# Layer-1 query and gate projections as 2x2 block products with seven half-products, keys and values through DRAM

## What is computed

```python
def window_gqa_layer(h_lat, h_ctx, w_in, sink, w_out, with_ctx_out):
    z = h_lat @ w_in                                  # 1024 x 1024 by 1024 x 2560
    q, k, v, g = z[..., :o1], z[..., o1:o2], z[..., o2:o3], z[..., o3:]
    q = axial_rope(q, cos_r, sin_r, cos_c, sin_c)
    k = axial_rope(k, cos_r, sin_r, cos_c, sin_c)
    zc = h_ctx @ w_in[:, o1:o3]                       # keys and values of the context
    ...                                               # scores in a window, softmax with a sink
    y_lat = (o * jax.nn.silu(g)) @ w_out
```

## Times and profile before

| | |
|---|---|
| three runs | 1406.67, 1405.72, 1405.45 us, median 1405.72 |
| profiled execution | span 1402.8 us from first to last instruction (no other time is listed for it) |
| TensorE | 1357.6 us busy, 97% |
| VectorE, ScalarE, GpSimd | 866.7, 730.4, 522.0 us busy |
| projections of layer 1 | 839.3 to 1072.5 us of the span |
| attention begins | 1076.2 us |

### The profile page before, as it was taken

How to read it: one execution, slowest core, us unless ns; L and a number is a source line. 1 busy time by engine, 2 the same in 40 slices (tenths; PEclk the granted TensorE clock), 3 DMA queues, 4 the chain that set the end, 5 groups by cost and what they waited for, 6 DMA issues and landing times. The chain is left out here.

```text
span 1402.8 us, 20174 instructions
## 1 busy us (share of the span) xinstructions
PE 1357.6 (97%) x7212; PEld 1153.9 (82%) x7212; DVE 866.7 (62%) x1250; ACT 730.4 (52%) x1150; POOL 522.0 (37%) x251
## 2 busy tenths in 40 slices
PE   5999999999999999999999999999998999999998
PEld 4788888888888888878888888888886788888786
DVE  7788968686868686892211154222213899998732
ACT  6475747474747474763222242222222899999421
POOL 0022222222232323212552533345433666667542
PEclk9999999999999999999999999999999999999999
DMA  9423131313131313264424443644357333242693
GB/s 373 155 89 119 61 103 60 103 60 103 60 103 60 103 60 103 87 229 151 135 90 135 158 157 114 157 135 124 101 153 222 124 100 98 82 142 68 193 269 116
DMA packets 94056, 177.18 MB, mean 126 GB/s; under 512 B 10384, under 2 KB 56496, under 8 KB 91696
## 3 DMA queue, kind: packets, MB, share of 16 engines
q1 hardware_dynamic: 94000, 176.44, 39.0%
HBM read 122.40 MB, written 44.06 MB: 119 GB/s over the span
## 5 line engine op out<-in xcount | busy, mean ns | idle before, releaser
L1031 PE MATMUL slab<-h_hi,w_hi 128*128 128x512 f32 x720 | 256.4, 356 | 3.0 <-DVE h_lo L372 2.3
L1032 PE MATMUL slab<-h_lo,w_hi 128*128 128x512 f32 x720 | 255.7, 355 | 0.0
L1033 PE MATMUL slab<-h_hi,w_lo 128*128 128x512 f32 x720 | 255.3, 355 | 0.0
L1003 POOL TENSOR_TENSOR w_lo<-wraw,w_hi 128x1024 fp32r<-128x1024 f32 x29 | 78.3, 2699 | 300.6 <-ACT w_hi L623 300.6
L2363 POOL TENSOR_TENSOR probs<-probs,rdenom 128x2560 f32<-128x2560 f32 (+1 forms) x32 | 135.7, 4242 | 53.6 <-DVE rdenom L2311 53.6
L1031 PEld LDWEIGHTS slab<-h_hi,w_hi 128*128 128x128 f32 x720 | 136.5, 190 | 22.9 <-DVE h_lo L372 2.6
L1033 PEld LDWEIGHTS slab<-h_hi,w_lo 128*128 128x128 f32 x720 | 136.5, 190 | 19.2
L1032 PEld LDWEIGHTS slab<-h_lo,w_hi 128*128 128x128 f32 x720 | 136.6, 190 | 18.9
L2000 PE MATMUL slab<-h_hi_c,w_hi 128*128 128x512 f32 x320 | 124.9, 390 | 0.5 <-POOL w_lo L1960 0.5
L2002 PE MATMUL slab<-h_hi_c,w_lo 128*128 128x512 f32 x320 | 124.5, 389 | 0.0
L2001 PE MATMUL slab<-h_lo_c,w_hi 128*128 128x512 f32 x320 | 124.5, 389 | 0.0
(11 more groups left out here) (345 smaller groups left out, 3189.6 us busy)
## 6 DMA issues: line engine op xcount, KB each, us to landing
wraw<-in_w_in SPq DMA_DIRECT2D x32, 512.0 KB, 3.4
wm<-in_wm SPq DMA_DIRECT2D x32, 512.0 KB, 3.6
mixT<-work SPq DMA_DIRECT2D x16, 640.0 KB, 4.0
wm<-in_wm SPq DMA_DIRECT2D x8, 1024.0 KB, 17.4
mraw<-mixT SPq DMA_DIRECT2D x16, 512.0 KB, 6.1
q_parts<-qT SPq DMA_DIRECT2D x32, 256.0 KB, 4.6
oT<-o_out SPq DMA_DIRECT2D x8, 1024.0 KB, 5.2
work<-in_xT SPq DMA_DIRECT2D x8, 640.0 KB, 8.3
```

Source lines behind the costliest of these rows:

```text
L1031: nc.tensor.matmul(out, l_hi, r_hi, start=start, stop=False)
L1032: nc.tensor.matmul(out, l_hi, r_lo, start=False, stop=False)
L1033: return nc.tensor.matmul(out, l_lo, r_hi, start=False, stop=stop)
```

## The change

**What it does.** The query and gate weights are taken in eight pairs of slabs (four of queries, four of gates). A pair is a 2x2 matrix of blocks: 2 slabs by 2 halves of the 1024 input features. h of the latents is one too: 2 halves of features by 2 halves of the tokens. Of the eight half-products (one block by one half: 4 tiles of features, 512 tokens, 12 matmuls) seven are made, in the order A11, A12, S2, S1, S3, S4, A22. Their operands are sums: on the weights' side S3 = A11-A21, S2 = A22-S3, S1 = S2+A11, S4 = A12-S2 for each pair; on h's side four sums T (16 pieces of 128x512 once). All sums are on GpSimd; each of the seven blocks and each T is split into hi (ScalarE) and lo (VectorE; before, GpSimd made the lo of weights).

TensorE adds products up in three PSUM banks of a pair; partial results are needed between two products, so ScalarE copies a bank (`take`) while TensorE waits with the next product into that bank, and VectorE adds other banks to the copies (`add_product`). The four results of a pair (each 128x512) are rotated, split and stored, or gated and stored, in halves.

Values come first now (slabs 0 and 1), are transposed group by group and stored to DRAM (`v`); attention fetches all of its values from there, the context's once, each block's window in turn. Keys are rotated after that and stored to DRAM (`kT`); `kd_hi`, `kd_lo` are loaded from it by 8 DMAs in pair 5 and 8 in pair 6. Before attention only block 0's queries are loaded. Buffers lie at other places.

**The core of the diff** (lines between the pieces are left out):

```diff
+        def half(p, i):
...
+            pe.wait_ge(bl.sem, bl.at + 7 * p + i + 1)
...
+            elif i == S2:
+                pe.wait_ge(cp.sem, cp.at + 4 * p + 1)
+                if p == 0:
+                    pe.wait_ge(tl.sem, tl.at + 16)
+            elif i == S3:
+                pe.wait_ge(cp.sem, cp.at + 4 * p + 2)
+            elif i == S4:
+                pe.wait_ge(cp.sem, cp.at + 4 * p + 3)
+            elif i == A22:
+                pe.wait_ge(cs.sem, cs.at + 3 * p + 2)
...
+        for p in range(PAIRS):
+            for i in (A11, A12, S2, S1, S3, S4, A22):
+                half(p, i)
```

ScalarE (`take` ends with cp, `finish_half` is the hi of a rotated half or a gate's tanh):

```diff
+        def take(k, bank, product):
+            p, j = k // 4, k % 4
+            act.wait_ge(pp.sem, pp.at + 7 * p + product)
...
+            else:
+                act.wait_ge(gst[j // 2], 32 * (p - Q_PAIRS))
...
+            for n in range(12, 16):
+                t_hi(n)
+            evict(2, 1)
...
+            for p in range(PAIRS):
+                more = p + 1 < PAIRS
+                k = 4 * p
+                if p > Q_PAIRS:
+                    finish_half(k - 2)
+                if p > 0:
+                    take(k - 1, 0, 7)
+                    block_hi(p, A22)
+                take(k, 0, 1)
+                if p == 0:
+                    rotated_hi(0)
...
+                if more:
+                    block_hi(p + 1, A12)
+                take(k + 2, 0, 3)
+                if more:
+                    block_hi(p + 1, S2)
+                if p == 0:
+                    rotated_hi(1)
+                finish_half(k)
+                take(k + 1, 1, 4)
```

VectorE and GpSimd:

```diff
+            for p in range(PAIRS):
...
+                block_lo(p, A22)
+                if p > 0:
+                    begin_half(k - 1)
+                    end_half(k - 1)
+                if more:
+                    block_lo(p + 1, A11)
+                if p == 0:
+                    rotate(1)
+                add_product(k, 2, 2, 1)
+                begin_half(k)
+                if more:
+                    block_lo(p + 1, A12)
+                if p == 0:
+                    add_rotated(1)
+                end_half(k)
...
+            sines(0)
+            rotated_lo(0)
+            sines(1)
+            for p in range(PAIRS):
...
+                if more:
+                    third_sum(p + 1)
+                if p == 0:
+                    second_sum(1)
+                    rotated_lo(1)
+                half_sines(k)
```

SyncE (KD_AT = 5; `load_x` waits for the lo of S4 of the pair before, `load_y` for that of A22):

```diff
+            for p in range(PAIRS):
+                if p + 1 < PAIRS:
+                    load_y(p + 1)
...
+                store_half(4 * p)
...
+                if p + 2 < PAIRS:
+                    load_x(p + 2)
+                if p in (KD_AT, KD_AT + 1):
+                    load_kd(p - KD_AT)
+                if p == QB_AT:
+                    load_first_block()
+                store_half(4 * p + 1)
```

Attention:

```diff
-                v = vs[:, LT + x - left, u, :]
...
+                v = v_ctx[:, x - left, u, :] if x >= left else vw[:, s, x, u, :]
```

More of the change, by code:

```diff
@@ L126, in out0_home, with laid_over @@
     return Home0(early, wo_a, junk, wo_b, mraw, x1, hb, m0, st, eps, wo_c, xn, xt, wo_d, gpb, m1, Y, TP)
-Home1 = namedtuple("Home1", "c_hi c_lo w_hi w_lo G kd_hi kd_lo wraw1 hraw2 C Z H R L vs slab VP q mask sink ident")
+Home1 = namedtuple("Home1", "c0_hi c0_lo c1 x_hi x_lo w_hi w_lo w_blocks t_parts kd_hi kd_lo wraw1 hraw2 raw_a vg C Z CK ZK R4 "
+                            "R_kv HK LK HQ LQ TG third slab VP q mask sink ident")
+def laid_over(nc, *buffers):
+    with ExitStack() as ctx:
+        return [ctx.enter_context(nc.sbuf_tensor(name, shape, dt)) for name, shape, dt in buffers]
 def proj1_home(nc):
+    KH = KT // 2
+    block, half = [P, 2, KH, P], [P, 512]
     with ExitStack() as ctx:
@@ new lines, in banks, with half_of, result, rotated @@
+    def banks(p):
+        return [slab[:, 3 * (p % 2) + i, :] for i in range(3)]
+    def half_of(k):
+        m, t = HALVES[k % 4]
+        return k // 4, 2 * (k // 4 % Q_PAIRS) + m, t
+    def result(k):
+        return home1.R4[:, k % 4, :] if k < 4 * Q_PAIRS else gates[:, k % 4, :]
+    def rotated(n):
+        if n < 2:
+            return R_kv[n][:, 0:N_LAT], CK[:], ZK[:], cos, sin
+        p, m, t = half_of(n - 2)
+        return result(n - 2), C[:, n % 2, :], Z[:, n % 2, :], cos[:, t * 512:(t + 1) * 512], sin[:, t * 512:(t + 1) * 512]
@@ new lines, in gate @@
+        def gate(k):
+            p, j = k // 4, k % 4
+            g = k - 4 * Q_PAIRS
+            if j == 3:
+                act.wait_ge(cp.sem, cp.at + k + 1)
+            else:
+                act.wait_ge(cs.sem, cs.at + 3 * p + j + 1)
+            if g < 2:
+                for done in qst:
+                    act.wait_ge(done.sem, done.at + 16 * 4 * Q_PAIRS)
+            else:
+                act.wait_ge(gg.sem, gg.at + g - 1)
+            nc.scalar.activation(TG[:, k % 2, :], result(k), ACT.Tanh, scale=0.5).then_inc(gt.sem, 1)
@@ L2200, in body @@
                 if is_block(b, NB - 3):
-                    sp.wait_ge(gst, 16 * KT)
+                    for stored in gst:
+                        sp.wait_ge(stored, 16 * KT)
                     sp.wait_ge(ost_s[0], 16)
```

834 lines of the change are left out of this document (553 added, 281 removed).

## The result

The changed kernel takes **1466.6 us** (median of 4 runs, 1465.2 to 1469.8), the kernel before 1405.6 on the same chip: a ratio of 1.0436 with a 95% interval of 1.0421 to 1.0450, 61 us slower. The forecast was 1455 with a range of 1421 to 1476. The profiled execution has a span of 1463.3 us, 60.5 above the 1402.8 of before.

What follows compares the result with a forecast made beforehand. TensorE, busy 97% of the span, was taken to bound the kernel. 71.3 us of added waits and costs less 21.7 of removed products gave +49.6; 1402.8 + 49.6 + 2.9 = 1455 us, range 1421 to 1476.

Steps and rivals of the forecast that it cites:

- before pair 0: Sums T and their lows ahead of the first query pair: 4 us of added time (0 to 8).
- pair 0 with its part of the clock: First query pair: TensorE waits 18.9 us at S4 for the copy after S1; a lower clock adds 2.8 us.
- pairs 1 to 3: Other query pairs: 27.2 us each, 8.2 over the 19.0 of products, three times: 24.6 us added.
- pair 4, pair 5: First two gate pairs: 7 us as the first copy waits for the last query sine, then 2 us.
- pairs 6 and 7: Last two gate pairs: copies wait for gate stores issued behind 8 key loads, 8 us and then 3 us.
- rival C: Query pairs: clock stays low (+11) or weight loads take longer behind two stores per query half; 1470 us, chance 0.13.
- The exclusion: Query pairs: GpSimd and two-SBUF-input VectorE instructions hold each other up, sharing one time, 15.5 + 9.0 = 24.5 us a pair.
- rival A: Projection pairs: VectorE and GpSimd are hardly held because they meet seldom; +17, 1423 us, chance 0.14.
- The 2.7 us that I added on top for the load of the second slab: Query pairs after the first: GpSimd's sums wait for the second weight slab, making 24.5 us into 27.2.
- 25.6; a gate store lands in 5.0 us, copy 0.6: Second-last gate pair: store issued behind key loads at 25.6 us, copy possible at 31.2, against 24.4 wanted: 6.8 us late.
- Cost 0: Attention: value windows from DRAM are as large and asked for as early as the SBUF transfers replaced; 0 us added.
- B: Projection pairs: GpSimd's half-size instructions take 0.9 us, copies come within their cover, gain kept; 1387 us, chance 0.05.

## Why the prediction was right, and where it was off

Measured against its own terms, from the stretches above (19.0 us a pair; sum 49.6 predicted, 60.5 measured):

| term | predicted | measured |
|---|---|---|
| removed | -21.7 | -21.7 |
| before pair 0 | 4 | 3.5 (62.7 against 59.2) |
| pair 0 with its part of the clock | 18.9 + 2.8 | 21.8 |
| pairs 1 to 3 | 24.6 | 19.4 |
| pair 4, pair 5 | 7, 2 | 5.8, 1.1 |
| pairs 6 and 7 | 8 + 3 | 26.2 |
| end of the projections | 1 | 0.7 |
| attention | 0 | 5.7 |

The measured terms add to 62.5; the keys' first product started 1.9 us earlier in this execution (837.33 against 839.27), which no term covers, and the last 0.1 is rounding. The 59.2 are the 233.1 us of all projections before, less the 173.9 of the queries and gates.

That the sum came so near is partly luck. Two terms were 20.9 us too small (pairs 6 and 7, attention) and five others together 8.1 too large, most of it in pairs 1 to 3. The measured 1466.6 is also nearer to rival C's 1470 than to the forecast's 1455; C's cause is answered below. TensorE's idle time from the first projection product to the last was forecast near 70 us; it is 58.0, and 20 more are products at the lower clock.

**The exclusion was right.** It decides the size and not the sign: pairs 1 to 3 lost 19.4 of the 60.5 us, and rival A, without it, was slower too. The rows, read in another part of the program, held in the pairs. The cuts of sines and of lows took 3.9 and 2.8 us a pair, the move of sines to VectorE 1.8, the early copies by themselves nothing. 24.5 us of shared time were counted, and the pairs took 25.5 on average (24.6, 26.8, 25.0). The 2.7 us that I added on top for the load of the second slab were the step that was too large: GpSimd waited for no transfer in pairs 1 to 3, only for VectorE's shuffles (20.0 us) and ScalarE's high parts (3.9). The count itself is a little high too: the shared instructions were under way for 23.0 us a pair, because one engine's follows the other's more closely than their lengths alone say (the addition above ended 0.54 us after the sum). The Trainium skill's rule (SBUF — State Buffer, section SBUF: two separate sides) says the same, for the two-input instructions of VectorE; the trace agrees, with VectorE's 1.53 to 1.83 us for a 128x512 beside GpSimd against 0.68, while additions that read PSUM kept to 0.68 and shuffles to 0.73.

**Pair 0 was right**: S4 started 32.7 us after A11, forecast 32.5, behind the copy after S1, itself behind the first query half's hi; the slow products behind the wait cost 2.7 us, forecast 2.8. The wait alone is 16.64 us and not 18.9, because the products ahead of it took longer: A11, at the lower clock behind a wait of 3.16 us, 4.43 us instead of 2.72. What the chain consists of was shown in part: moving the keys' and the halves' sines to VectorE took 7.4 us, cutting the halves' sines alone nothing that can be told.

**Pairs 6 and 7 were off by 15 us.** The step that failed: "25.6; a gate store lands in 5.0 us, copy 0.6". I priced the keys ahead of the store by their issue (0.96 us each from the earlier trace rows, an issue time of another form of DMA; here 0.6) and then let the store land as if the queues were empty. Its bytes stood behind 2.56 MB, 10.9 us at the 235 GB/s or so that the queues moved while the keys passed. Spreading the loads, which changes no issue time, took 19.5 us out of the two pairs; issuing the store first took out nothing. Pair 7 I took for a smaller case of the same, 3 us, although mask and first queries stand there behind the second 8 loads; it was the same again, 11.7. And each long wait drew products at the lower clock: of the 26.2 us 20.2 are waits and 6.0 are slow products; I had this in pair 0 only.

**Attention was off by 5.7 us.** The step that failed: "Cost 0". I weighed what the window's transfer costs and how early it is asked for, and not what its new place on SyncE holds up: at block NB - 3 the wait for products of values now stands ahead of the mixed tiles' load, which is issued at 1314.5 us where GpSimd wants the tiles at 1318.3 (1324.14 less the 5.87 of its wait). The order of SyncE's issues in attention's last blocks was to be read, as it was for the key loads in pair 5.

**The clock** lay as predicted in time that is waited for, in pairs 1 to 3: keeping it up changed 76.42 us to 76.16. In pairs 6 and 7, where a transfer sets the wait, no run kept it up, so whether the 6.0 us would come back there is open. Rival A (hardly held) and B (gain kept) are refuted by the pairs' 25.5 us; rival C named the clock and slower weight loads, and neither is the cause: between the stores of query halves the loads of 512 KB landed in 4.0 and 4.9 us, sooner than before. Its 1470 was near the time for another reason, the gate stores.

## What to carry to other kernels

Before work is taken off a TensorE that is busy all the time and given to VectorE and GpSimd, add up VectorE's instructions with two SBUF inputs and all of GpSimd's as one time, not as two. Here that sum foretold a query pair to within 2.3 us (24.5 for 25.5, 21.7 for 21.5 to 24.0) as long as both engines had much of it; with nearly all work on VectorE the other sum was the bound, VectorE's own list and the time in which it stands still for GpSimd (18.8 + 5.2 for 24.7). A store that someone waits for costs the bytes that were issued ahead of it, divided by the rate of the queues, so large loads go between such stores in small portions. And where a condition on one transfer changes, read what stands behind it in the same engine's list, in every block where it now holds.

## What was not expected of the hardware

A GpSimd 128x512 with a constant and one input takes 1.49 us, longer than a two-input product or subtraction of that size, 1.26 to 1.29. And 16.64 us of waiting at one product were no 16.64 us of gain: with the copies taken earlier the wait moved from S4 to A22 and into the next pair, and of the 117 us of pairs 0 to 3 3 went, which pair 4 took back.
